# Ten of twelve pairs of token tiles: xn transposed on VectorE in 32x32 squares instead of on TensorE

## The chip, the cores and the metric

One core of one Trainium2 chip. The metric is the device time of one execution in microseconds (us).

## The reference, cut to what matters

An encoder block on 2048 + 1024 tokens of 1024 channels, all in float32. What matters here lies between the mixing and the FFN:

```
x = x + concat(ya, yb) @ w_out
h = rmsnorm(x, norm2_g)                      # x * rstd(x) * norm2_g
x = x + (silu(h @ w_gate) * (h @ w_up)) @ w_down     # D_FF = 2816
```

`rmsnorm` takes the mean square over the 1024 channels of a token; `norm2_g` is one weight per channel.

## The kernel before, in words

Every float32 matmul is three matmuls of rounded parts (hi x hi, lo x hi, hi x lo; lines 351 to 353, `three_products`). The rounded part is made by ScalarE, the rest by VectorE (`round_...` and `rest_of_...`). Large products use a scheme of seven products instead of eight (sums of halves before, sums of products after), so that both the weights and the moving data are needed as seven combinations.

The output projection (`project_out`) works on 24 tiles of 128 tokens. The first four tiles are done plainly; from then on two tiles are a pair, n = 2 to 11, and one pair is seven products of twelve matmuls (`pair`, `seventh`) on TensorE, in the order A11, S1, S2, A12, S3, S4, A22. The loop over pairs is written out by hand for each engine (`in_turn`, with pair LAST = 11 apart). While the products of pair n run, VectorE and ScalarE

- add the products of pair n to x (`u_sums`, `c11`, `c22`, `c12`, `c21`) in `x1`, which SP stores to `x1_scr` and fills anew with x for the next pair but one,
- prepare the seven combinations of y for pair n + 1 (`sum_v`, `round_v`, `rest_of_v`),
- and make h of pair n - 1. This is the part that the change is about: ScalarE squares a tile of x1 with its row sum (`squares`), VectorE and ScalarE make rstd from it (`variance`, `root`, `inverse`; lines 1835, 1623, 359 to 365), ScalarE writes xn = x1 * rstd (`scaled`, line 1627), TensorE transposes xn in eight squares of 128 into two PSUM banks (`transposes`, line 2020), ScalarE copies them to `h_out` and multiplies by norm2_g, which is one number per partition there (`stage_h`, line 1637), VectorE makes four sums of h's halves (`combine`, lines 1849 to 1854), and SP stores seven half-rows of h to `ha_scr` (`store_h`, lines 1529 to 1531).

Each engine runs its own instructions in the order in which they are written, and waits on semaphores. SP issues all of these DMAs, in its own order: per pair a store of x1, the load of y, a load of x, the second store of x1, the second load of x, and the stores of h. A load of x waits for the store of the same slot of x1 to have landed (`next_x`).

The FFN (`ffn`) reads seven 128x2048 blocks `a_raw` from `ha_scr` for each of three blocks of 1024 tokens, splits them into a_hi and a_lo (lines 2401 and 2592), and uses them as moving operand of 21 rounds of products. Its first tile is interleaved with the last pair of the output projection (`feed`).

Of the kernel before, what the change touches and what calls it, by code (L numbers as in the profile page):

```python
# [151 lines left out]
class Ahead:  # L152
# [4 lines left out]
    def __init__(self, nc, ctx):  # L157
# [699 lines left out]
class Mixer:  # L857
# [136 lines left out]
    def load_small(self, sp):  # L994
# [80 lines left out]
def mix(nc, ctx, ahead, mixer, z_scr, y_scr, w_pool):  # L1075
# [107 lines left out]
    def scalar(act):  # L1183
# [57 lines left out]
        for n in range(N):  # L1241
# [169 lines left out]
def project_out(nc, ctx, ahead, mixer, y_scr, x, x1_scr, ha_scr):  # L1411
# [19 lines left out]
    eye, gain2 = ahead.eye1, ahead.gain2  # L1431
# [35 lines left out]
    x1_stored, h_stored = ahead.x1_stored, ahead.h_stored  # L1467
# [35 lines left out]
    def sync(sp, feed):  # L1503
# [80 lines left out]
        store_h(LAST - 1, 0)  # L1584
# [3 lines left out]
        store_h(LAST, 1)  # L1588

    def scalar(act, feed):  # L1590
# [30 lines left out]
        def root(m, slot):  # L1621
            act.wait_ge(var_ready, m + 1)
            act.activation(std[:, slot:slot + 1], var[:, slot:slot + 1], ACT.Sqrt).then_inc(std_ready, 1)

        def scaled(m, slot):
            act.wait_ge(rstd_chain, m * 4 + 4)
            act.activation(xn[:, slot % 2, :], x1[:, slot, :], ACT.Copy, scale=rstd[:, slot:slot + 1]).then_inc(xn_ready, 1)  # L1627

        def stage_h(m, slot, stored=None):

            for half in range(2):
                act.wait_ge(transposed, m * 2 + (half + 1))
                if half == 0 and stored is not None:
                    act.wait_ge(*stored)
                for i in range(4):
                    d = 4 * half + i
                    out = act.activation(h_out[:, slot % 2, d, :], t_ps[(slot % 2) * 2 + half][:, i, :], ACT.Identity,  # L1637
                                         scale=gain2[:, d:d + 1])
                out.then_inc(h_staged, 1)
# [11 lines left out]
        act.wait_ge(ahead.gains_loaded, 2 * DMA)  # L1651
# [3 lines left out]
        root(0, 0)  # L1655
# [5 lines left out]
        root(1, 1)  # L1661
# [3 lines left out]
        stage_h(1, 1)  # L1665
# [1445 lines left out]
```

## Time and profile before

| | us |
|---|---|
| median of 3 runs | 2491.96 (2491.36 to 2492.42) |
| profiled execution, its own time | 2491.23 |
| its span | 2489.4 |
| TensorE busy (PE) | 2474.7 (99%) |
| VectorE busy (DVE) | 1676.6 (67%) |
| ScalarE busy (ACT) | 965.2 (39%) |

The page's 40 slices are 62.2 us each; the pairs of the output projection lie in slices 6 to 9 (375 to 557 us). TensorE's granted clock is 1.00 of full speed in every stretch shown. PE is TensorE, PEld its weight loads, SPq the queue of DMAs that SP issues. "Busy" of a matmul counts its whole duration, and matmuls overlap: one lasts 389 ns, and the next starts 227 ns after it.

### The profile page before, as it was taken

The page shows a single profiled execution, that of the slowest core. Times are in us where ns is not written, and L with a number is a line of the kernel's source. Part 1 is how long each engine was busy: PE and PEld are TensorE (multiplying, and loading weights), DVE is VectorE, ACT ScalarE, POOL GpSimd, SP SyncE. Part 2 cuts the span into 40 slices and gives each one's busy share as a digit, 9 for nine tenths or more (in the row PEclk, how much of TensorE's full clock was granted, in tenths as well). Part 3 has the DMA queues.
Part 4 walks back from the last instruction along what each step waited for, and adds up shares of the span by engine and source line. Part 5 has one row for each costly group of instructions (what it writes and reads, how often), then busy time and mean ns, then how long its engine had stood idle before and what let it go on. Part 6 is the DMA issues. An engine that isn't in the chain of part 4 may idle for free.

```text
span 2489.4 us, 32156 instructions
## 1 busy us (share of the span) xinstructions
PE 2474.7 (99%) x11141; PEld 2049.1 (82%) x11141; DVE 1676.6 (67%) x2600; ACT 965.2 (39%) x1830; POOL 166.9 (7%) x222
## 2 busy tenths in 40 slices
PE   9999999999999999999999999999999999999998
PEld 7888878887888888888888888888888888888887
DVE  5555788779767767877677687666774564455565
ACT  5534566667333333433333343333332232233333
POOL 2555400000000000000000000000000000000000
PEclk9999999999999999999999999999999999999999
DMA  6433767666423222532232432232346654354554
GB/s 184 115 85 99 223 221 254 238 238 260 157 80 116 97 103 110 195 113 110 80 126 101 155 146 96 110 110 89 118 186 217 242 200 168 119 196 149 195 189 148
DMA packets 154373, 381.99 MB, mean 153 GB/s; under 512 B 11992, under 2 KB 48184, under 8 KB 145076
## 3 DMA queue, kind: packets, MB, share of 16 engines
q1 hardware_dynamic: 145616, 350.81, 40.8%
q0 software_dynamic: 8240, 29.94, 3.2%
q8 instruction: 51, 0.84, 0.1%
q14 instruction: 34, 0.28, 0.0%
q10 hardware_dynamic: 432, 0.14, 0.0%
HBM read 254.22 MB, written 126.62 MB: 153 GB/s over the span
## 4 chain that ended last, share of the span: by engine, by line
PE 85%; DVE 2%; ACT 1%; issue 0%; DMA 0%; DVEq 0%
PE bank L351 28%; PE bank L353 28%; PE bank L352 28%; PE bank L2020 1%; ACT a_hi L2401 0%; DVE a_lo L2592 0%; DMA a_raw<-ha_scr 0%; PE bank L1373 0%; PE bank L1059 0%; DVE x L1818 0%; ACT h_out L1637 0%; DVE scratch L1033 0%; DVE zy_late L1044 0%; DVE uv_lo L1071 0%; ACT xn L1627 0%
## 5 line engine op out<-in xcount | busy, mean ns | idle before, releaser
L351 PE MATMUL bank<-a_hi,w_hi 128*128 128x512 f32 x1848 | 719.4, 389 | 2.0 <-DVE w_lo L2603 1.6
L352 PE MATMUL bank<-a_lo,w_hi 128*128 128x512 f32 x1848 | 718.9, 389 | 0.0
L353 PE MATMUL bank<-a_hi,w_lo 128*128 128x512 f32 x1848 | 718.9, 389 | 0.0
L351 PEld LDWEIGHTS bank<-a_hi,w_hi 128*128 128x128 f32 x1848 | 346.9, 188 | 75.6 <-DVE w_lo L2603 2.8
L353 PEld LDWEIGHTS bank<-a_hi,w_lo 128*128 128x128 f32 x1848 | 347.0, 188 | 72.0
L352 PEld LDWEIGHTS bank<-a_lo,w_hi 128*128 128x128 f32 x1848 | 347.0, 188 | 71.7
L351 PE MATMUL bank<-t_hi,s_hi 128*128 128x512 f32 x924 | 359.4, 389 | 0.0
L352 PE MATMUL bank<-t_lo,s_hi 128*128 128x512 f32 x924 | 359.4, 389 | 0.0
L353 PE MATMUL bank<-t_hi,s_lo 128*128 128x512 f32 x924 | 359.4, 389 | 0.0
L2414 ACT ACTIVATE w_hi<-t_raw 128x512 fp32r<-128x512 f32 x256 | 162.3, 634 | 462.4 <-PE bank L353 378.8
L2753 DVE TENSOR_TENSOR s_lo<-s_raw,s_hi 128x512 fp32r<-128x512 f32 x231 | 156.2, 687 | 230.7 <-ACT s_hi L2489 230.7
L2489 ACT ACTIVATE s_hi<-s_raw 128x512 fp32r<-128x512 f32 x231 | 133.8, 621 | 317.1 <-DMA s_raw<-s_scr 312.9
L351 PEld LDWEIGHTS bank<-t_hi,s_hi 128*128 128x128 f32 x924 | 173.4, 188 | 36.0
L353 PEld LDWEIGHTS bank<-t_hi,s_lo 128*128 128x128 f32 x924 | 173.4, 188 | 36.0
L352 PEld LDWEIGHTS bank<-t_lo,s_hi 128*128 128x128 f32 x924 | 173.4, 188 | 36.0
L2603 DVE TENSOR_TENSOR w_lo<-t_raw,w_hi 128x512 fp32r<-128x512 f32 x256 | 176.0, 688 | 29.9 <-ACT w_hi L2414 26.2
L2603 DVE TENSOR_TENSOR w_lo<-w_raw,w_hi 128x512 fp32r<-128x512 f32 x192 | 132.2, 688 | 87.7 <-ACT w_hi L2414 87.6
L2414 ACT ACTIVATE w_hi<-w_raw 128x512 fp32r<-128x512 f32 x192 | 120.6, 628 | 121.3 <-PE bank L353 121.0
L351 PE MATMUL bank<-h_hi,win_hi 128*128 128x512 f32 x380 | 149.6, 394 | 0.0
L353 PE MATMUL bank<-h_hi,win_lo 128*128 128x512 f32 x380 | 148.0, 389 | 0.0
L352 PE MATMUL bank<-h_lo,win_hi 128*128 128x512 f32 x380 | 148.0, 389 | 0.0
L2374 POOL DMA_DIRECT2D acc<-x_scr x6 | 4.5, 752 | 1641.1 <-PE bank L353 1641.1
(277 smaller groups left out, 3163.1 us busy)
## 6 DMA issues: line engine op xcount, KB each, us to landing
s_scr<-sums_out SPq DMA_DIRECT2D x33, 1792.0 KB, 5.9
s_raw<-s_scr SPq DMA_DIRECT2D x42, 1024.0 KB, 5.0
w_raw<-in_w_gate SPq DMA_DIRECT2D x64, 512.0 KB, 3.5
w_raw<-in_w_up SPq DMA_DIRECT2D x64, 512.0 KB, 4.3
wd_staged<-in_w_down SPq DMA_DIRECT2D x121, 256.0 KB
a_raw<-ha_scr SPq DMA_DIRECT2D x21, 1024.0 KB, 5.0
s_raw<-s_scr SPq DMA_DIRECT2D x21, 768.0 KB, 4.4
x<-in_x SPq DMA_DIRECT2D x24, 512.0 KB, 4.9
```

Source lines behind the costliest of these rows:

```text
L351: pe.matmul(out, w_hi, m_hi, start=first, stop=False, **checks)
L352: pe.matmul(out, w_hi, m_lo, start=False, stop=False, **checks)
L353: return pe.matmul(out, w_lo, m_hi, start=False, stop=last, **checks)
L2020: mm = pe.transpose(t_ps[(slot % 2) * 2 + k][:, i, :], xn[:, slot % 2, d * P:(d + 1) * P], eye[:, :])
L2374: pool.dma_start(acc[b][half][:, :, :], src).then_inc(acc_loaded[b][half], DMA)
L2414: act.activation(w_hi[j][:, :], src, ACT.Copy).then_inc(w_hi_done, 1)
L2489: act.activation(s_hi[c][:, k - 4 * c, :], s_raw[c][:, k - 4 * c, :], ACT.Copy).then_inc(s_hi_done, 1)
L2603: dve.tensor_tensor(w_lo[j][:, :], src, w_hi[j][:, :].bitcast(F32), ALU.subtract).then_inc(w_ready, 1)
L2753: dve.tensor_tensor(s_lo[c][:, k - 4 * c, :], s_raw[c][:, k - 4 * c, :], s_hi[c][:, k - 4 * c, :].bitcast(F32), ALU.subtract).then_inc(s_r ...
```

## The change

For pairs 1 to 10 (all but the first and the last) TensorE no longer transposes xn. After both tiles of a pair are scaled, VectorE transposes xn into `h_out`, one operation of 128x512 for each tile and half of the channels (`turn_squares`). It transposes each 32x32 square in its place, so partition 32 i + f of `h_out` holds channels of f, and tokens of the i-th group of 32. The columns are taken so that within `h_out` a partition's row holds, for each group m of 32 channels, four runs of 32 tokens. norm2_g is then one number per partition and square: ScalarE multiplies `h_out` in place by `gain_squares`, in 32 operations of 2 x 32 columns (`gains`). The stores of h bring the squares to their rows: one DMA for each group of 32 partitions and part, in pieces of 128 floats, twelve DMAs per pair instead of three (`store_squares`). `ha_scr` has its first two dimensions swapped. Inside a row of 512 the tokens now stand in another order, and the FFN reads its moving operand with a stride that undoes it (`tokens_of`). rstd is made for both tiles of a pair at once (`variance`, `root`, `inverse` on two columns), which goes with both `scaled` moving next to each other. `combine` moves to the end of a pair's work on VectorE. The first pair's h and the last pair's are still transposed by TensorE, and staged in the new token order. `gain_squares` is loaded early by four small DMAs.

```diff
@@ ScalarE @@
-        def stage_h(m, slot, stored=None):
+        def gains(n, a, first, last):
+            act.wait_ge(transposed, turned(n, a))
+            for b in range(first, last):
+                m, k = divmod(b, 4)
+                d = 4 * a + k
+                both = h_out[:, :, 4 * a + m, k * SQUARE:(k + 1) * SQUARE]
+                out = act.activation(both, both, ACT.Identity, scale=gain_squares[:, m, d:d + 1])
@@ ScalarE, pair @@
             round_v(after, k_after, 1 - par, A11)
-            scaled(n * 2 - 1, slot + 1)
-            stage_h(n * 2 - 2, slot, (h_stored[par], k * (3 * DMA)))
+            scaled(n, slot)
+            scaled(n, slot + 1)
             round_v(after, k_after, 1 - par, S1)
-            stage_h(n * 2 - 1, slot + 1)
-            for v in (S2, A12, S3):
-                round_v(after, k_after, 1 - par, v)
+            gains(n - 1, 0, 0, 16)
+            round_v(after, k_after, 1 - par, S2)
+            gains(n - 1, 1, 0, 8)
+            round_v(after, k_after, 1 - par, A12)
+            gains(n - 1, 1, 8, 16)
+            round_v(after, k_after, 1 - par, S3)
             squares(n * 2, 2 * par, n * 4 + 3)
             round_v(after, k_after, 1 - par, S4)
-            root(n * 2, 2 * par)
@@ ScalarE, last pair @@
-        round_v(LAST, NT // 4 - 1, 1, A22)
-        scaled(NT - 4, 0)
+        norms(LAST, NT // 4 - 1, 1)
+        scaled(LAST, 0)
+        scaled(LAST, 1)
         act.wait_ge(y_ready, split(LAST, A22))
         feed.round_a(0, 0)
-        squares(NT - 3, 1, LAST * 4)
-        root(NT - 3, 1)
-        copy_product(LAST)
-        scaled(NT - 3, 1)
-        stage_h(NT - 4, 0, (h_stored[1], (NT // 4 - 1) * (3 * DMA)))
+        gains(LAST - 1, 0, 0, 16)
         act.wait_ge(pair_ready, product_of(LAST, 2))
         feed.round_a(0, 1)
         feed.round_w(0, 0, 0, 0)
-        stage_h(NT - 3, 1)
+        gains(LAST - 1, 1, 0, 16)
@@ VectorE @@
+        def turn_squares(n, a, tile):
+            if (a, tile) == (0, 0):
+                dve.wait_ge(halves_out, halves_stored(n - 1))
+            if a == 0:
+                dve.wait_ge(xn_ready, n * 2 + (tile + 1))
+            half = xn[:, tile, a * HALF:(a + 1) * HALF].rearrange("p (k m f) -> p m k f", m=ROWS, f=SQUARE)
+            done = dve.transpose(h_out[:, tile, 4 * a:4 * a + 4, :].rearrange("p m (k t) -> p m k t", t=SQUARE), half)
+            if tile:
+                done.then_inc(transposed, 1)
@@ VectorE, last pair @@
-        c21(LAST - 1, 0)
-        for v in (A22, S3, S4):
-            rest_of_v(LAST, 1, v)
+        norms(LAST, 1)
         feed.rest_of_a(0, 0)
-        variance(NT - 3, 1)
-        inverse(NT - 3, 1)
+        for a in range(2):
+            for tile in range(2):
+                turn_squares(LAST - 1, a, tile)
         u_sums(LAST, rounds, 1)
@@ SP @@
-            sp.dma_start(ha_scr[0:2, b, :, q, :].rearrange("i p c -> p i c"), even).then_inc(h_stored[par], DMA)
-            sp.dma_start(ha_scr[2, b, :, q, :], odd).then_inc(h_stored[par], DMA)
-            sp.dma_start(ha_scr[3:7, b, :, q, :].rearrange("i p c -> p i c"), sums[:, :, :]).then_inc(h_stored[par], DMA)
+            for i in range(ROWS):
+                rows, cols = slice(i * SQUARE, (i + 1) * SQUARE), slice(i * P, (i + 1) * P)
+                sp.dma_start(ha_scr[b, 0:2, :, q, cols].rearrange("a (m f) c -> f (a m) c", f=SQUARE),
+                             h_out[rows, 0, :, :]).then_inc(halves_out, DMA)
+                sp.dma_start(ha_scr[b, 2, :, q, cols].rearrange("(m f) c -> f m c", f=SQUARE),
+                             h_out[rows, 1, 4:, :]).then_inc(halves_out, DMA)
+            sp.wait_ge(h_combined, n * 4 + 4)
+            for i in range(ROWS):
+                rows, cols = slice(i * SQUARE, (i + 1) * SQUARE), slice(i * P, (i + 1) * P)
+                sp.dma_start(ha_scr[b, 3:7, :, q, cols].rearrange("v (m f) c -> f (v m) c", f=SQUARE),
+                             h_sums[0][rows, :, :].rearrange("f v (m c) -> f (v m) c", m=ROWS)).then_inc(sums_out, DMA)
@@ TensorE @@
-            transposes(n * 2 - 2, slot)
             ready(S2, T2)
             seventh(S2)
-            transposes(n * 2 - 1, slot + 1)
@@ FFN, TensorE @@
+        def tokens_of(a, k):
+            return a[:, :, :].rearrange("p q (i k t) -> p (q i) k t", i=ROWS, t=SQUARE)[:, :, k, :]
-                mm = three_products(pe, ps[:, :], w_hi[j][:, cols], w_lo[j][:, cols], a_hi[slot][:, :, cols],
-                                    a_lo[slot][:, :, cols], k == 0 and not more, k == 3, skip_group_check=more)
+                mm = three_products(pe, ps[:, :], w_hi[j][:, cols], w_lo[j][:, cols], tokens_of(a_hi[slot], k),
+                                    tokens_of(a_lo[slot], k), k == 0 and not more, k == 3, skip_group_check=more)
```

The order of VectorE's instructions at the start of pair 3, before, from the last v_lo of pair 3's own combinations to `u_sum` (var, std, tmp and rstd are the steps of rstd, y_raw, v_raw and v_lo belong to the combinations of y for the next pair, bank1 and bank2 to the products of pair 3):

```order
L1780 TENSOR_TENSOR v_lo5_175<-v_raw5_182,v_hi5_168 128x512
L1835 TENSOR_SCALAR var3_151<-sumsq3_150 128x1
L359 RECIPROCAL tmp3_153<-std3_152 128x1
L361 SCALAR_TENSOR_TENSOR rstd3_154<-tmp3_153 128x1
L363 TENSOR_TENSOR rstd3_154<-rstd3_154,var3_151 128x1
L365 SCALAR_TENSOR_TENSOR rstd3_154<-rstd3_154,tmp3_153 128x1
L1780 TENSOR_TENSOR v_lo0_170<-y_raw0_51,v_hi0_163 128x512
L1775 TENSOR_TENSOR v_raw1_178<-y_raw0_51 128x512
L1775 TENSOR_TENSOR v_raw2_179<-v_raw1_178,y_raw0_51 128x512
L1780 TENSOR_TENSOR v_lo1_171<-v_raw1_178,v_hi1_164 128x512
L1800 TENSOR_TENSOR u_sum_184<-bank1,u_sum_184 128x512
```

and of the change, the same place:

```order
L1877 TENSOR_SCALAR var3_152<-sumsq3_151 128x2
L360 RECIPROCAL tmp3_154<-std3_153 128x2
L362 SCALAR_TENSOR_TENSOR rstd3_155<-tmp3_154 128x2
L364 TENSOR_TENSOR rstd3_155<-rstd3_155,var3_152 128x2
L366 SCALAR_TENSOR_TENSOR rstd3_155<-rstd3_155,tmp3_154 128x2
L1822 TENSOR_TENSOR v_lo0_171<-y_raw0_51,v_hi0_164 128x512
L1890 STREAM_TRANSPOSE h_out_98<-xn_148 128x512
L1817 TENSOR_TENSOR v_raw1_179<-y_raw0_51 128x512
L1890 STREAM_TRANSPOSE h_out_98<-xn_148 128x512 x3
L1817 TENSOR_TENSOR v_raw2_180<-v_raw1_179,y_raw0_51 128x512
L1822 TENSOR_TENSOR v_lo1_172<-v_raw1_179,v_hi1_165 128x512
L1842 TENSOR_TENSOR u_sum_185<-bank1,u_sum_185 128x512
```

Four transposes now stand ahead of `u_sum`, one before and three after v_raw1; the chain of rstd here works on two columns, and the other chain of a pair, which stood at its end, is gone (the four sums of h stand there now). SP, the stores of h of one pair and the DMA on either side, before:

```order
L1509 DMA x_96<-in_x 128x1024
L1529 DMA ha_scr<-h_out 128x2x512
L1530 DMA ha_scr<-h_out 128x512
L1531 DMA ha_scr<-h_sums_148 128x4x512
L1513 DMA x_scr<-x_96 128x1024
```

and of the change (the first two stores stand four times in turn):

```order
L1527 DMA x_97<-in_x 128x1024
L1557 DMA ha_scr<-h_out 32x8x128
L1559 DMA ha_scr<-h_out 32x4x128
L1564 DMA ha_scr<-h_sums_149 32x16x128 x4
L1531 DMA x_scr<-x_97 128x1024
```

Twelve stores stand where three stood, and the next store of x1 is behind them.

## Rows read from the trace of the kernel before

**Rows 1.** The page: busy us of each engine, share of the span, instructions

```profile
PE 2474.7 (99%) x11141; PEld 2049.1 (82%) x11141; DVE 1676.6 (67%) x2600; ACT 965.2 (39%) x1830; POOL 166.9 (7%) x222
```

**Rows 2.** By stretch: length, busy PE, PEld, DVE, ACT, POOL, clock, DMA share, GB/s

```profile
477.34:498.20 20.86, 20.86 (x103) 17.42 (x102) 16.43 (x35) 13.43 (x33) 0.00 (x0) 1.00 0.73 252
...
600.00:610.00 10.00, 8.69 (x46) 6.74 (x44) 9.93 (x10) 10.00 (x19) 0.00 (x0) 1.00 0.80 316
```

**Rows 3.** Timeline of TensorE: start us, us, engine, line, what

```profile
477.34 0.47 PE L351 MATMUL bank<-wout_hi,v_hi 128*128 128x512 f32 x1
...
485.63 0.39 PE L351 MATMUL bank<-wt_hi,v_hi 128*128 128x512 f32 x1
...
488.35 0.39 PE L351 MATMUL bank<-wout_hi,v_hi 128*128 128x512 f32 x1
...
498.20 0.47 PE L351 MATMUL bank<-wout_hi,v_hi 128*128 128x512 f32 x1
```

**Rows 4.** Timeline of VectorE in one pair

```profile
478.06 0.68 DVE L1800 TENSOR_TENSOR u_sum<-bank,u_sum 128x512 f32<-128x512 f32 x1
478.78 0.69 DVE L1802 TENSOR_TENSOR u_sum<-bank,u_sum 128x512 f32<-128x512 f32 x1
...
480.59 0.68 DVE L1810 TENSOR_TENSOR x<-x,u_sum 128x512 f32<-128x512 f32 x1
...
488.03 0.15 DVE L1835 TENSOR_SCALAR var<-sumsq 128x1 f32<-128x1 f32 x1
...
489.60 0.69 DVE L1818 TENSOR_TENSOR x<-bank,x 128x512 f32<-128x512 f32 x1 [0.21 <-DVE rstd L365]
```

**Rows 5.** VectorE's transposes of the first stage; weight loads (ns, min/median/max) of TensorE's

```profile
60.31 3.10 DVE L636 STREAM_TRANSPOSE x_turned<-xin 128x512 f32<-128x512 f32 x3
...
L718 PEld LDWEIGHTS bank<-eye,xin x16: 197/204/212, 18.9 to 29.1; 128*128 128x128 f32 x16
...
L2020 PEld LDWEIGHTS bank<-eye,xn x192: 138/140/143, 360.2 to 605.2; 128*128 128x128 f32 x192
```

**Rows 6.** Timeline of ScalarE in one pair; [idle before <- what ended it]

```profile
473.96 2.17 ACT L1637 ACTIVATE h_out<-bank,gain 128x128 f32<-128x128 f32 x8
...
486.24 0.63 ACT L1615 ACTIVATE v_hi<-v_raw 128x512 fp32r<-128x512 f32 x1 [5.22 <-DVE v_raw L1775]
...
492.19 0.20 ACT L1623 ACTIVATE std<-var 128x1 f32<-128x1 f32 x1 [0.57 <-DVE var L1835]
492.30 0.58 ACT L1643 ACTIVATE u_sum<-bank 128x512 f32<-128x512 f32 x1
493.30 1.14 ACT L1627 ACTIVATE xn<-x,rstd 128x1024 f32<-128x1024 f32 x1
```

**Rows 7.** Timeline of SP's DMA issues; two stretches, columns as rows 2

```profile
72.63 5.24 SPq L435 DMA_DIRECT2D xin<-in_x  x8
...
484.44 0.37 SPq L1529 DMA_DIRECT2D ha_scr<-h_out  x1
...
485.36 0.71 SPq L1531 DMA_DIRECT2D ha_scr<-h_sums  x1
...
491.88 0.33 SPq L1509 DMA_DIRECT2D x<-in_x  x1
...
75.00:79.50 4.50, 4.50 (x21) 3.72 (x20) 0.63 (x1) 4.50 (x23) 2.61 (x5) 1.00 1.22 226
583.00:589.00 6.00, 6.00 (x28) 4.94 (x27) 5.78 (x8) 4.47 (x11) 0.00 (x0) 1.00 1.02 408
```

**Rows 8.** Timeline of VectorE in the last pair

```profile
572.75 0.69 DVE L1818 TENSOR_TENSOR x<-bank,x 128x512 f32<-128x512 f32 x1
...
581.10 0.69 DVE L1800 TENSOR_TENSOR u_sum<-bank,u_sum 128x512 f32<-128x512 f32 x1 [1.70 <-PE bank L353]
...
584.51 2.29 DVE L2592 TENSOR_TENSOR a_lo<-a_raw,a_hi 128x2048 fp32r<-128x2048 f32 x1 [0.18 <-ACT a_hi L2401]
```

**Rows 9.** The page's costliest groups: matmuls of the FFN (busy us, mean ns)

```profile
L352 PE MATMUL bank<-a_lo,w_hi 128*128 128x512 f32 x1848 | 718.9, 389 | 0.0
```

More of the change, by code:

```diff
@@ L1247, in scalar @@
                 if SIDE[a] == "wp":
-                    act.wait_ge(ahead.gains_loaded, 2 * DMA)
+                    act.wait_ge(ahead.gains_loaded, (2 + ROWS) * DMA)
                 if SIDE[a][0] != "G":
@@ L1519, in next_x, with store_turned @@
             load_x(m + 4, slot)
-        def store_h(n, par):
-            last = isinstance(n, int) and n == LAST
+        def store_turned(n):
+            last = n == LAST
             b, q = n // 4, n % 4
@@ L1619, in squares, with root, scaled, stage_h @@
             act.activation(xn[:, slot % 2, :], x1[:, slot, :], ACT.Square, accum_out=sumsq[:, slot:slot + 1]).then_inc(squares_done, 1)
[L1621 to L1626, printed above, removed]
+        def root(number, tiles):
+            act.wait_ge(var_ready, number + 1)
+            act.activation(std[:, tiles], var[:, tiles], ACT.Sqrt).then_inc(std_ready, 1)
+        def scaled(number, slot):
+            act.wait_ge(rstd_chain, number * 4 + 4)
             act.activation(xn[:, slot % 2, :], x1[:, slot, :], ACT.Copy, scale=rstd[:, slot:slot + 1]).then_inc(xn_ready, 1)
-        def stage_h(m, slot, stored=None):
+        def stage_h(banks_done, tile):
             for half in range(2):
[L1632 to L1637, printed above, removed]
-                                         scale=gain2[:, d:d + 1])
+                act.wait_ge(transposed, banks_done + half + 1)
+                for k in range(4):
+                    d = 4 * half + k
+                    out = act.activation(h_out[:, tile, 4 * half:4 * half + 4, k * SQUARE:(k + 1) * SQUARE],
+                                         t_ps[2 * tile + half][:, k, :].rearrange("p (i t) -> p i t", t=SQUARE), ACT.Identity,
+                                         scale=gain2[:, d:d + 1])
+                out.then_inc(h_staged, 1)
+        def gains(n, a, first, last):
[5 more added lines that the diff above has]
+                out = act.activation(both, both, ACT.Identity, scale=gain_squares[:, m, d:d + 1])
+            if (a, last) == (1, 16):
                 out.then_inc(h_staged, 1)
@@ L1650, in scalar @@
         round_y(1)
-        act.wait_ge(ahead.gains_loaded, 2 * DMA)
+        act.wait_ge(ahead.gains_loaded, (2 + ROWS) * DMA)
         round_y(2)
@@ L1676, in norms @@
             round_v(n, k, par, A22)
-            scaled(n * 2 - 2, slot)
             squares(n * 2 - 1, slot + 1, n * 4)
-            root(n * 2 - 1, slot + 1)
+            root(n, slice(slot, slot + 2))
             copy_product(n)
@@ L1917, in pair @@
             c11(n, par)
-            if isinstance(n, int) and n == 2:
-                c22(n, par)
-                combine(n - 1, (h_stored[par], k * (3 * DMA)))
-            else:
-                combine(n - 1, (h_stored[par], k * (3 * DMA)))
-                c22(n, par)
+            c22(n, par)
             rest_of_v(after, 1 - par, A12)
@@ L1975, in combine_last @@
         def combine_last():
-            combine(LAST, None, last=True)
+            combine(LAST, staged(LAST - 1) + 4, last=True)
         feed.second_tile(combine_last)
@@ L2011, in products, with transposes @@
             mm.then_inc(tile_ready, 1)
-        def transposes(m, slot, first=False):
+        def transposes(m, tile):
             pe.wait_ge(xn_ready, m + 1)
             for k in range(2):
-                if not first:
-                    pe.wait_ge(h_staged, m * 2 + (k - 3))
                 for i in range(4):
                     d = 4 * k + i
-                    mm = pe.transpose(t_ps[(slot % 2) * 2 + k][:, i, :], xn[:, slot % 2, d * P:(d + 1) * P], eye[:, :])
+                    mm = pe.transpose(t_ps[2 * tile + k][:, i, :], xn[:, tile, d * P:(d + 1) * P], eye[:, :])
                 mm.then_inc(transposed, 1)
@@ L2069, in tensor @@
         products(1)
-        transposes(0, 0, first=True)
+        transposes(0, 0)
         products(2)
-        transposes(1, 1, first=True)
+        transposes(1, 1)
         products(3)
```

144 lines of the change are left out of this document (84 added, 60 removed).

## Prediction

> **What bounds the kernel now.** I read the page first: TensorE is busy 99% of the span [rows 1]. A change pays only if it takes work from TensorE, and only while nothing else then ends later. Next, the stretches of the output projection (about 340 to 557 us): in one pair of token tiles TensorE is busy for all of 20.86 us, VectorE for 16.43, ScalarE for 13.43, and the DMA engines have a share of 0.73 [rows 2]. The reader is to see there that three other resources have little room. The timeline of TensorE gives the parts of a pair: the same product starts at 477.34 and at 498.20, 20.86 us apart, and twelve matmuls (one of seven products) take 485.63 to 488.35, 2.72 us [rows 3]. Seven make 19.04 us; the remaining 1.82 us are the two sets of eight transposes of xn. Last, the stretch 600 to 610, where VectorE is busy 9.93 of 10 us, ScalarE 10.00, TensorE 8.69 [rows 2]: from the last pair into the first tile of the FFN the other two engines set the pace, so work given to them there is paid in full.
>
> **TensorE.** The transposes of ten pairs go, 160 of them: at most 10 x 1.82 = 18.2 us.
>
> **VectorE, per pair.** It now runs 24 operations of 512 columns. They start 0.60 us apart (three between 478.78 and 480.59), and 0.72 in the two places where one waits for its predecessor (478.06 to 478.78) [rows 4]: 22 x 0.60 + 2 x 0.72 = 14.6 us. It also runs two chains for rstd, the one shown from 488.03 to the next work at 489.60 [rows 4], 1.5 us each. The change keeps one chain (two columns at a time) and adds four transposes. Their price decides the case. Upper end: the transposes of the first stage have the same 128x512 shape, and three of them in a row take 3.10 us [rows 5], 1.03 each. But those read every fourth float of a row; the new ones read runs of 32 floats. Lower end: 0.60 apart, as any operation of 512 columns [rows 4]. That reading every fourth float costs an engine something is seen on TensorE: the weight loads of transposes take 204 ns from xin, read that way, and 140 ns from xn, read in one run [rows 5]. In reading, the new transposes are nearer to the contiguous operations, so I take 0.63 apart (0.71 long) and keep 1.03 for a rival. The Trainium skill says (Vector Engine (DVE) Microarchitecture Reference, 3.8) that the transpose array sustains one element per cycle per lane; by that the 1.03 would be due to the reading, and the sum would be mine. The trace of before has no transpose of contiguous data to show it.
>
> Sum: 14.6 + 1.5 + 4 x 0.63 = 18.6 us, and 0.45 of waiting, since both scaled tiles now come one after the other from ScalarE (1.14 each [rows 6], started 1.05 apart) and only one short operation lies between: 19.1 us, level with TensorE's 19.04. So a pair should take about 19.1 us.
>
> **ScalarE, per pair.** Sixteen copies of h out of PSUM go: eight of them take 2.17 us [rows 6], 0.27 each, 4.3 us. One root goes (0.1). In come 32 multiplications of 2 x 32 columns. Bounds: 0.11 (a root of one column, 492.19 to 492.30) and 0.27 (128 columns) [rows 6], so 3.5 to 8.7 us; about halfway, 0.2, gives 6.4. ScalarE comes to 13.4 + 2.0 = 15.4 of 19.1 us. They stand between the roundings that feed the next pair's products, in places where ScalarE idled 5.22 us before [rows 6]; that idle time covers the 2.0 us. At 0.27 it would no longer, and `combine`, behind them on VectorE, would hold up the next pair.
>
> **SP and the DMA queues, per pair.** h leaves in pieces of 512 B instead of 2 KB, and in twelve DMAs of 32 partitions instead of three of 128. Issuing: of the three, the first takes 0.37 and the largest 0.71 us; eight loads of xin, which have this form, take 5.24 us, 0.66 each [rows 7]. Eight smaller ones and four of that size are some 6 us of SP, 4.5 more; SP has room for it. Transfer: during the xin loads the engines move 226 GB/s at a share over 1, with another load of larger pieces among them; with large pieces alone 408 GB/s [rows 7]. I take 205 for the small ones. So the 1.83 MB of h (seven blocks of 128 x 512 floats) take 8.9 us instead of 4.5. The other 3.15 MB of a pair take 7.7. That is 16.6 of 19.1 us. But SP issues in order and waits twice per pair for a store of x1 before it reloads the slot. Before, stores of 2.36 MB issued from 484.44 on (5.8 us at 408 GB/s) let the waiting load go at 491.88 [rows 7], 7.44 us later: 1.6 us of landing. The loop now is: h 8.9, store of x1 1.3, landing 1.6, then 2.1 MB (y, x, second store) 5.1, landing 1.6, issue 0.4: 18.9 us. It is as long as the pair. I put 1 to 1.5 us in all on it. The other bound for unseen stores of this form: no dearer than the loads (gain kept), or a quarter slower (a rival). 
>
> **The tail.** There VectorE sets the pace. Before, c21 starts at 572.75, u_sum at 581.10 and the second a_lo at 584.51 [rows 8], 8.35 and 11.8 us later. Now the rounding of `a` stands behind both scaled tiles: c21 and three v_lo 2.4 us, rstd chain to 3.9, two xn to 6.0, a_hi (twice the columns of an xn, 1.9 as an estimate) to 7.9, a_lo (2.29 [rows 8], the next starts 0.1 before its end) to 10.2, four transposes to 12.7. So u_sum comes 12.7 us after c21 instead of 8.35. On ScalarE sixteen multiplications (3.2) and the next a_hi (1.9) follow the second transpose at 11.5, so the second a_lo starts at 16.6 instead of 11.8: 4.8 us lost. The last pair's removed transposes gain nothing here, as TensorE is ahead. So nine pairs count: 9 x 1.8 = 16.2 gained, 4.9 lost, 1 to 1.5 for the queue: **-10 us**. The new order of h's columns inside a row changes TensorE's moving operand of the FFN from runs of 128 floats to runs of 32; I cost it at nothing, since matmuls that read runs of 128 floats (a_lo [rows 9]) and of 512 (wt_hi, 485.63 [rows 3]) take 389 and 390 ns. A nanosecond on each of the 5,544 matmuls would be 5.5 us.
>
> The profiled execution is 2491.23 us (span 2489.4 and 1.8 around it), 0.7 under the median of 2491.96, against which I state everything: **2482 us**.
>
> **The rivals.**
> - A, the forecast: 2479 to 2486. Chance 0.40.
> - B, the store queue becomes the bound: h stores at 190 GB/s take 9.7 us, the loop 19.7, so 0.6 us a pair over nine pairs: 2487; at 170 GB/s the gain is gone, 2498. For it: the loop has no slack. Against it: 16.6 us of transfer in 19.1 is still not full. Chance 0.18.
> - C, on the other side: the new transposes cost what the old ones do, 1.03 each. VectorE then needs 14.6 + 1.5 + 4.1 + 0.45 = 20.65 us a pair and takes TensorE's place; a pair gains 0.2 us, nine pairs 2, and the tail loses 4.9 and 4 x 0.4 = 1.6 more: +4.5, 2496. It decides from about 0.9 us apart, where nine pairs of 20.86 - 16.55 - 4 x 0.9 no longer pay the tail. For it: the only measured transposes. Chance 0.33.
> - D, on the other side too, and by more: stores in 512 B pieces run slower than such loads. From 170 GB/s down they take back all; at 150 they need 12.2 us for h, loop 22.2, so 1.35 us a pair more than before over nine pairs, and the tail: +17, 2509. No row shows these stores. Chance 0.06.
> - E, the FFN's matmuls read slower, 3 ns each: 16.6 us lost against 10 gained, 2499. Chance 0.03.
> That the change does not do what it says is excluded by the order of instructions: the transposes stand on VectorE there.
>
> **How the numbers follow.** A measurement of this kernel tells about 0.2%, 5 us, from no change. Faster: nearly all of A (0.38) and half of B (0.10). Within 5 us: the rest of A and B (0.10), and most of C (0.24). Slower: the upper part of C (0.09), D and E. The range from 2478 to 2500 takes in A, B and C; A alone would be 2479 to 2486.
>
> **What would show it.** In the timeline of VectorE the new transposes start 0.63 apart (A, B) or 1.03 (C). A product of TensorE recurs every 19.1 us (A), with TensorE idle for 0.5 us or more before the products that wait for u_sum in C, and with VectorE's idle time ended by x or by the h stores in B. Multiplications of 64 columns last 0.15 to 0.25 us. The stretch of a pair shows a DMA share near 0.9. From the last pair's start to 620 the profile is some 5 us longer. The forecast is wrong if a pair lasts over 20 us, whatever the cause, or if FFN matmuls stand more than 227 ns apart.

## The result, and the profile after

| | us |
|---|---|
| median before | 2491.66 |
| median after | 2548.07 (2546.15 to 2552.46) |
| ratio | 1.0229, interval 1.0211 to 1.0246 |
| profiled execution after, its own time | 2552.46 |
| its span | 2550.7 |

The change makes the kernel 56 us slower. The forecast was 2482 us, 10 faster, and the range ended at 2500. The profiled execution is the slowest of the four, 4.4 us over the median, so the parts found in its trace add up to more than 56 us. The page's first part and the costliest matmul groups, which answer to [rows 1] and [rows 9]:

```profile
PE 2519.5 (99%) x10981; PEld 2036.2 (80%) x10981; DVE 1696.1 (66%) x2590; ACT 994.2 (39%) x1980; POOL 166.6 (7%) x222
...
L352 PE MATMUL bank<-a_hi,w_hi 128*128 128x512 f32 x1848 | 738.7, 400 | 0.9 <-DVE w_lo L2653 0.9
L354 PE MATMUL bank<-a_hi,w_lo 128*128 128x512 f32 x1848 | 738.6, 400 | 0.0
L353 PE MATMUL bank<-a_lo,w_hi 128*128 128x512 f32 x1848 | 735.9, 398 | 0.0
...
L353 PE MATMUL bank<-t_lo,s_hi 128*128 128x512 f32 x924 | 359.4, 389 | 0.0
```

TensorE is 99% busy in both kernels, and this is the trap of the page: its 160 removed instructions are gone from the count, and yet it is busy 45 us longer. The FFN's matmuls that read `a` went from 389 ns to 398 and 400; those of the last product, which do not read `a` (t_lo), kept 389. The stretch from 640 to 1000 us, all FFN, by windows (columns as in [rows 2]), after:

```profile
640.00:1000.00 360.00, 360.00 (x1523) 286.09 (x1522) 242.49 (x372) 109.18 (x181) 0.00 (x0) 1.00 0.27 98
```

and before:

```profile
640.00:1000.00 360.00, 360.00 (x1590) 298.19 (x1589) 252.72 (x389) 113.81 (x189) 0.00 (x0) 1.00 0.29 106
```

In the same 360 us at the same clock, 1,523 matmuls run instead of 1,590: one each 236.4 ns instead of 226.4. Over 5,544 matmuls, 10.0 ns are 55 us.

Splitting the 61.3 us between the two spans at the same instruction of both traces gives the account. The first u_sum of pair 2 starts at 397.00 (before 394.52), that of pair 10 at 560.23 (561.40), the FFN's first matmul at 600.3 (592.6), its last hi x hi matmul that reads `a` at 1914.9 (1853.7):

| stretch | forecast | measured |
|---|---|---|
| up to pair 2 | 0 | +2.5 |
| eight pairs, from pair 2 to pair 10 | 8 x -1.8 = -14.4 | -3.7 |
| pair 10 to the FFN's first matmul | +4.9 - 1.8 + 1 to 1.5 (queue) | +8.9 |
| FFN matmuls that read `a` | 0 | +53.5 |
| the rest | 0 | +0.1 |

The +2.5 us up to pair 2 are no more than executions differ by: the kernels of e4 and e12 below, which up to there are the kernel before, start pair 2 at 396.43 and 394.72. The second and third row vary too: e1 and e3 below, whose pairs are this kernel's, have -6.2 and -5.8 over the eight pairs and +7.7 and +7.4 behind them.

A pair recurs every 20.40 us (163.23 us over eight), not 19.1. The first two pairs last 19.36 and 19.29 us; from the third on it is 20.1 to 20.5, and 22.5 for the eighth. VectorE's timeline at the start of a pair:

```profile
490.62 0.69 DVE L1822 TENSOR_TENSOR v_lo<-y_raw,v_hi 128x512 fp32r<-128x512 f32 x1 [0.25 <-ACT v_hi L1649]
492.88 0.71 DVE L1890 STREAM_TRANSPOSE h_out<-xn 128x512 f32<-128x512 f32 x1 [1.57 <-DMA ha_scr<-h_out]
493.52 0.65 DVE L1817 TENSOR_TENSOR v_raw<-y_raw 128x512 f32<-128x512 f32 x1
494.09 1.89 DVE L1890 STREAM_TRANSPOSE h_out<-xn 128x512 f32<-128x512 f32 x3
```

Three transposes take 1.89 us: 0.60 apart and 0.7 long. They cost what I took them for. But the first waits 1.57 us until the previous pair's h has landed. SP's queue in the same pair:

```profile
479.55 0.43 SPq L1531 DMA_DIRECT2D x_scr<-x  x1
486.11 0.33 SPq L1527 DMA_DIRECT2D x<-in_x  x1
486.49 0.43 SPq L1557 DMA_DIRECT2D ha_scr<-h_out  x1
...
490.55 3.24 SPq L1564 DMA_DIRECT2D ha_scr<-h_sums  x4
493.83 0.70 SPq L1531 DMA_DIRECT2D x_scr<-x  x1
...
499.29 0.34 SPq L1527 DMA_DIRECT2D x<-in_x  x1
499.67 0.43 SPq L1531 DMA_DIRECT2D x_scr<-x  x1
```

and the chain that ended last, in the same stretch:

```profile
473.30 5.80 DMA x_scr<-x
...
479.55 6.50 DMA x_scr<-x
...
493.83 5.39 DMA x_scr<-x
...
499.67 6.64 DMA x_scr<-x
```

SP's loop in one pair (479.55 to 499.67, 20.1 us) is two landings of x1, 6.5 and 5.4 us, between them 7.3 us of issuing twelve stores, and 0.9 us of reloads and gaps. In it SP waits for nothing but landings. These landings are not longer than before the change: between 375 and 557 us the median from issue to landing of a store of x1 is 6.3 us, and was 6.9. New are the 7.3 us of issuing in line with them, where the three stores took 1.6 us (484.44 to 486.07). The first stores of h could have gone 3.4 us before 486.49, when ScalarE's last multiplication of h ended at 483.12, but they stand behind a reload that waits for a landing:

```profile
481.11 2.01 ACT L1681 ACTIVATE h_out<-h_out,gain_squares 128x64 f32<-128x64 f32 x8
```

In the last pair the waits between 560 and 600 us (total, times, longest), and one stretch of it by windows:

```profile
DVE a_lo L2642 <- ACT a_hi L2451: 9.4, 2, 5.3
PE bank L352 <- DVE x L1860: 7.6, 1, 7.6
PE bank L352 <- DVE u_sum L1844: 4.9, 2, 3.0
...
ACT a_hi L2451 <- DMA a_raw<-ha_scr: 3.6, 1, 3.6
```

```profile
590.00:595.00 5.00, 0.00 (x0) 0.00 (x0) 3.48 (x4) 4.43 (x13) 0.00 (x0) 0.50 1.02 428
```

The load of a_raw stands behind the twelve stores, ScalarE's a_hi waits for it, VectorE stands in `a_lo`'s wait for a_hi, and TensorE waits 7.6 us for the x that is queued behind. With TensorE idle, its granted clock is 0.50 there (1.2 GHz), and the timeline of TensorE goes on with matmuls of 0.63 us instead of 0.39, some 0.43 apart, so an idle stretch of TensorE is paid a second time:

```profile
595.15 0.77 PE L352 MATMUL bank<-wt_hi,v_hi 128*128 128x512 f32 x1 [7.56 <-DVE x L1860]
...
596.14 0.63 PE L354 MATMUL bank<-wt_hi,v_lo 128*128 128x512 f32 x1
596.57 0.63 PE L352 MATMUL bank<-wt_hi,v_hi 128*128 128x512 f32 x1
```

The twelve matmuls from 595.15 on take 5.2 us instead of 2.7. The same happens after the wait of 3.0 us for u_sum: the granted clock from 563 to 566 us is 0.50, with matmuls of 0.63 us. The kernel before has no such stretch here.

### The profile page after: what moved, and what is told of

The parts are those of the page before. It is cut to its first block, busy times and chain, and to the rows that moved or that the text cites. A ratio compares the mean times of both kernels' runs of the same rounds, so it can differ in the third digit from the quotient of the medians.

```text
span 2550.7 us, 31996 instructions
## 1 busy us (share of the span) xinstructions
PE 2519.5 (99%) x10981; PEld 2036.2 (80%) x10981; DVE 1696.1 (66%) x2590; ACT 994.2 (39%) x1980; POOL 166.6 (7%) x222
## 4 chain that ended last, share of the span: by engine, by line
PE 78%; DMA 4%; SPq 3%; DVE 2%; ACT 1%; issue 1%; DVEq 0%
PE bank L354 26%; PE bank L352 26%; PE bank L353 26%; DMA x_scr<-x 4%; SPq L1564 1%; SPq L1559 1%; SPq L1557 1%; ACT h_out L1681 0%; DMA w_raw<-in_w_up 0%; DVE a_lo L2642 0%; PE bank L1377 0%; SPq L1527 0%; PE bank L1063 0%; DVE v_lo L1822 0%; DVE zy_late L1048 0%
## 5 line engine op out<-in xcount | busy, mean ns | idle before, releaser
L352 PE MATMUL bank<-a_hi,w_hi 128*128 128x512 f32 x1848 | 738.7, 400 | 0.9 <-DVE w_lo L2653 0.9
L354 PE MATMUL bank<-a_hi,w_lo 128*128 128x512 f32 x1848 | 738.6, 400 | 0.0
L353 PE MATMUL bank<-a_lo,w_hi 128*128 128x512 f32 x1848 | 735.9, 398 | 0.0
L353 PEld LDWEIGHTS bank<-a_lo,w_hi 128*128 128x128 f32 x1848 | 348.4, 189 | 90.0
L354 PEld LDWEIGHTS bank<-a_hi,w_lo 128*128 128x128 f32 x1848 | 347.2, 188 | 90.6
L353 PE MATMUL bank<-t_lo,s_hi 128*128 128x512 f32 x924 | 359.4, 389 | 0.0
L354 PE MATMUL bank<-t_hi,s_lo 128*128 128x512 f32 x924 | 359.4, 389 | 0.0
L353 PEld LDWEIGHTS bank<-t_lo,s_hi 128*128 128x128 f32 x924 | 173.4, 188 | 36.0
L354 PEld LDWEIGHTS bank<-t_hi,s_lo 128*128 128x128 f32 x924 | 173.4, 188 | 36.0
L354 PE MATMUL bank<-h_hi,win_lo 128*128 128x512 f32 x380 | 148.0, 389 | 0.0
L353 PE MATMUL bank<-h_lo,win_hi 128*128 128x512 f32 x380 | 147.9, 389 | 0.0
```

Of the source, the lines that this page charges most:

```text
L352: pe.matmul(out, w_hi, m_hi, start=first, stop=False, **checks)
L353: pe.matmul(out, w_hi, m_lo, start=False, stop=False, **checks)
L354: return pe.matmul(out, w_lo, m_hi, start=False, stop=last, **checks)
```

## The experiments

Medians of "before" in these groups of runs are 2492.4 to 2492.5. All runs but e3, e10 and e11 give the FFN its tokens or channels in the wrong order (e8 leaves out weights too), so they compute another result and stand here for their time alone. The edits are shown in part: `...` marks what is left out, and semaphore increments are left out throughout.

**Which part costs the 56 us.** Two theories: R, reading the moving operand in runs of 32 floats; S, something else in the FFN. e1 undoes the reading alone, e2 does it alone.

```diff
@@ e1, in the change @@
-    tokens_of(a_hi[slot], k), tokens_of(a_lo[slot], k)
+    a_hi[slot][:, :, cols], a_lo[slot][:, :, cols]
@@ e2, in the kernel before @@
-    a_hi[slot][:, :, cols], a_lo[slot][:, :, cols]
+    tokens_of(a_hi[slot], k), tokens_of(a_lo[slot], k)
```

> The changed kernel, but the FFN's matmuls read 512 floats in four runs of 128, as before; the rows still hold the new token order, so the blocks of 128 channels are mixed and the FFN's result is another one. Everything ahead of the FFN and its DMAs is as in the change. Theory R (reading the moving operand in 16 runs of 32 floats costs 10 ns a matmul, x 5,544 = 55 us): about 2493 us, FFN matmuls 227 ns apart. Theory S (something else slows the FFN's matmuls, such as the other traffic, the clock, or later operands): 2546 us or little less, still 237 ns apart.

> The kernel before, in which only the FFN's matmuls read their 512 floats in 16 runs of 32 at a distance of 128 (each takes floats of four blocks of channels, so the FFN's result is another one). Theory R: 2492 + 55 = 2547 us, matmuls 237 ns apart, nothing else changed. Theory S: 2492.

Measured: e1 2494.68 us (ratio to before 1.001, 1.000 to 1.002), e2 2546.52 (1.0218, 1.0201 to 1.0235). That is 53.4 us less than the change and 54.1 more than before. The stretch from 640 to 1000 us of e1, then of e2:

```profile
640.00:1000.00 360.00, 360.00 (x1590) 298.38 (x1589) 253.47 (x391) 114.09 (x190) 0.00 (x0) 1.00 0.29 105
```

```profile
640.00:1000.00 360.00, 360.00 (x1522) 286.82 (x1522) 243.34 (x374) 109.27 (x182) 0.00 (x0) 1.00 0.27 99
```

The reading alone is the cause, in either kernel, and the whole rest of the change is worth +2 us (0 to 5 by the interval).

**How the price depends on the run.** The kernel before with runs of 64 (e4) and of 16 (e12); only `t` in `tokens_of` differs.

> The kernel before, in which the FFN's matmuls read 8 runs of 64 floats at a distance of 256 (the FFN's result is another one). If each run costs a fixed time beyond the first: four runs cost nothing visible against one (389 and 390 ns), 16 cost 10 ns, so 12 more runs cost 0.83 ns each and 8 runs 3.3 ns: 2492 + 18 = 2510 us. If there is a threshold between 32 and 128 floats: 2492 or 2547.

> The kernel before, in which the FFN's matmuls read 32 runs of 16 floats at a distance of 64 (the FFN's result is another one). Runs of 64 cost nothing, runs of 32 cost 9.8 ns a matmul. If a run costs a fixed time and part of it is hidden: 16 more runs cost more than the 9.8 ns, at 0.6 to 1.2 ns a run 20 to 30 ns in all, 2600 to 2655 us. If any run under 64 floats costs one fixed step per matmul: 2547 again.

Measured: e4 2492.51 us (0.9999, 0.999 to 1.0009), e12 2579.32 (1.035, 1.0333 to 1.0368). The window 640 to 1000 of e4, then of e12:

```profile
640.00:1000.00 360.00, 360.00 (x1590) 298.10 (x1589) 253.51 (x391) 114.20 (x190) 0.00 (x0) 1.00 0.29 105
```

```profile
640.00:1000.00 360.00, 360.00 (x1485) 281.12 (x1484) 236.45 (x362) 106.57 (x177) 0.00 (x0) 1.00 0.26 96
```

Eight runs of 64 floats: nothing. Sixteen of 32: 9.8 ns a matmul (54.1 us / 5,544). Thirty-two of 16: 15.7 ns (86.8 / 5,544). So it is neither a fixed time per run (e4 would be 2510, and e12 at least 2600) nor one step below 64 (e12 would be 2547). The straight line by the number of runs fell on both sides; a threshold between 32 and 128 floats is what e4 showed, and e12, which matched neither of its expectations, shows that the price below it still grows. The length of a run, the number of runs and the distance between them (256, 128 and 64 floats) changed together in these three runs, so which of them sets the price is not shown; "runs of 32" below stands for the whole pattern.

**Can the reading be mended cheaply.** e3: ScalarE reads a_raw in runs of 32 and writes a_hi in token order; a_lo is made in the place of a_raw and stays in the other order.

```diff
-    act.activation(a_hi[s][:, :, :], a_raw[s][:, :, :], ACT.Copy)
+    act.activation(in_order(a_hi[s]), by_block(a_raw[s]), ACT.Copy)
...
-    tokens_of(a_hi[slot], k), tokens_of(a_lo[slot], k)
+    in_order(a_hi[slot])[:, k, :, :], tokens_of(a_lo[slot], k)
```

> The changed kernel, with ScalarE writing a_hi in token order (it reads a_raw in runs of 32 and writes one run), so that two of three FFN matmuls read 512 floats in one run and only those of a_lo (1,848) read runs of 32. Theory R, cost by matmul and by reading: 2548 - 3,696 x 0.010 = 2511 us, a_hi matmuls 227 ns and a_lo matmuls 237 ns apart from the next; ScalarE's rounding of a block stays at 1.9 us if it reads runs of 32 for nothing. If the cost hung on the weights or on the sequence instead of on each matmul's own reading: 2548 or 2493.

Measured: 2524.10 us (1.0129, 1.0112 to 1.0146), 13 more than expected. The groups:

```profile
L353 PE MATMUL bank<-a_lo,w_hi 128*128 128x512 f32 x1848 | 737.3, 399 | 0.0
L354 PE MATMUL bank<-a_hi,w_lo 128*128 128x512 f32 x1848 | 729.4, 395 | 0.0
L352 PE MATMUL bank<-a_hi,w_hi 128*128 128x512 f32 x1848 | 723.1, 391 | 1.6 <-DVE w_lo L2665 1.5
...
L2463 ACT ACTIVATE a_hi<-a_raw 128x2048 fp32r<-128x2048 f32 x21 | 39.8, 1910 | 18.1 <-PE bank L354 13.2 <-DMA a_raw<-ha_scr 4.8
```

ScalarE reads runs of 32 for nothing (1,910 ns on average, and 1,910 without the edit). On TensorE, one third of the strided reads keeps 29.4 us of 53.4 (against e1), 15.9 ns each: the strided matmul (L353) lasts 399 ns instead of 389, and the one behind it (L354) 395, though it reads one run. Thinning out such reads pays less than in proportion.

**What holds a pair at 20.4 us.** Theory Q, the store queue (rival B of the prediction), against theory E, the hand-overs between VectorE and ScalarE (not the prediction's rival E). All on the kernel of e1. e5 stores h in three DMAs as before; e6 keeps twelve DMAs of 32 partitions, but in pieces of 2 KB; e8 leaves out 29 of the 32 multiplications.

```diff
@@ e5: store_squares @@
-    for i in range(ROWS): ...
+    sp.dma_start(ha_scr[b, 0:2, :, q, :].rearrange("i p c -> p i c"), even)
+    sp.dma_start(ha_scr[b, 2, :, q, :], odd)
...
+    sp.dma_start(ha_scr[b, 3:7, :, q, :].rearrange("i p c -> p i c"), h_sums[0][:, :, :])
@@ e6: store_squares, in the loop over i @@
+    even = h_out[rows, 0, :, :].rearrange("p (a k) c -> p a (k c)", a=2)
+    sp.dma_start(ha_scr[b, 0:2, rows, q, :].rearrange("i p c -> p i c"), even)
...
@@ e8: gains @@
-    for b in range(first, last):
+    for b in range(last - 1, last):
```

> The kernel of e1_read_runs_128 (2494.7 us, a pair 20.5 us), with h of the ten pairs stored as before the change: three DMAs of 128 partitions in pieces of 2 KB (the squares then lie in the wrong rows). Theory Q (a pair is bounded by the stores of h and what waits behind them: the halves' landing for the transposes, the landing of x1 for the reload): a pair 19.1 to 19.4 us, 9 x 1.2 = 11 us less, 2484; in the last pair the loads of a come earlier too, 2 to 4 us more, 2481. Theory E (VectorE and ScalarE set the pair through their hand-overs): 20.5 us a pair, 2494.

> The kernel of e1_read_runs_128, with the twelve DMAs of 32 partitions kept, but each in pieces of 2 KB instead of 512 B (the squares lie in the wrong rows). If the number of DMAs and their 32 partitions are what costs (issuing 7.3 us of SP): as e1, 2494. If it is the piece of 512 B: as e5, 2481 to 2484. Between them if both.

> The kernel of e1_read_runs_128, with three of the 32 multiplications by norm2_g per pair kept (the others are left out, so h lacks the weight in most squares). ScalarE then does 7 us less per pair. Theory Q or L: h is ready earlier, but SP issues its stores after the reload of x, so a pair stays at 20.3 to 20.5 us, 2492 to 2494. Theory E (ScalarE's 8 us of multiplications hold up the combinations of the next pair): 19.1 to 19.5 us, 2482 to 2486.

Measured (a pair of e1 is 20.09 us, the mean of eight between 19.3 and 21.1): e5 2485.68 us (0.9973, 0.9963 to 0.9983), a pair 19.32, each of the eight within 0.1; e6 2494.20 (1.0008, 0.9998 to 1.0018), a pair 20.13; e8 2495.23 (1.0013, 1.0003 to 1.0022), a pair 20.06. The queue holds the pair, ScalarE's new work does not, although it is 7 us of it. The piece of 512 B is not what costs: e6 moves pieces of 2 KB and is as slow as e1. From the second store of x1 to its reload, SP's rows of e5 and then of e6:

```profile
471.70 0.43 SPq L1531 DMA_DIRECT2D x_scr<-x  x1
477.03 0.33 SPq L1527 DMA_DIRECT2D x<-in_x  x1
```

```profile
476.86 0.43 SPq L1531 DMA_DIRECT2D x_scr<-x  x1
484.43 0.33 SPq L1527 DMA_DIRECT2D x<-in_x  x1
```

5.3 us and 7.6 (in the next pair 5.4 and 6.7). The twelve DMAs also issue for 7 us in line with the landings, where e5 needs 1.2, and that is the larger part. Which of the two, the number of DMAs or their 32 partitions, lengthens this landing was not parted. The Trainium skill (SBUF — State Buffer, Door 1: The DMA port swizzle) says that 32 partitions reach 8 of the 16 ports; no run here shows whether that plays a part.

**Latency or traffic.** e7 keeps every DMA of e1 and changes SP's order: both reloads of x first, then the next x1 even, h, x1 odd, each when its data is ready.

```diff
@@ SP, pair @@
-    store_x1(2 * n - 2, slot)
     sp.wait_ge(y_ready, split(n, A22))
...
     next_x(2 * n - 2, slot, before + 1)
-    store_x1(2 * n - 1, slot + 1)
     next_x(2 * n - 1, slot + 1, before + 1)
+    store_x1(2 * n, 2 * par)
     store_squares(n - 1)
+    store_x1(2 * n + 1, 2 * par + 1)
...
+store_x1(2, 2)
+store_x1(3, 3)
 for n in range(2, LAST):
...
-store_x1(NT - 4, 0)
-store_x1(NT - 3, 1)
```

> The kernel of e1_read_runs_128, with the same DMAs in another order on SP: both reloads of x ahead of the stores of h, and the two stores of x1 of the next pair around them, each where its data is ready (x1 even, h, x1 odd). Nothing on SP then waits for a landing behind h's stores. Theory L (latency: the loop of landings is too long, not the traffic): a pair 19.1 to 19.4 us, 2482 to 2484. Theory W (bandwidth: pieces of 512 B fill the queues): 20.3 us a pair, 2492 to 2494.

Measured: 2485.76 us (0.9974, 0.9964 to 0.9984), a pair 19.33. One pair of e7 by windows, SP's start of the stores, and VectorE at the transposes:

```profile
493.45:512.75 19.30, 19.30 (x85) 15.63 (x84) 17.97 (x35) 16.48 (x49) 0.00 (x0) 1.00 0.83 259
```

```profile
500.06 0.33 SPq L1531 DMA_DIRECT2D x_scr<-x  x1
500.44 0.42 SPq L1557 DMA_DIRECT2D ha_scr<-h_out  x1
...
504.76 2.98 SPq L1564 DMA_DIRECT2D ha_scr<-h_sums  x4
507.78 1.18 SPq L1531 DMA_DIRECT2D x_scr<-x  x1
```

```profile
488.22 0.69 DVE L1822 TENSOR_TENSOR v_lo<-y_raw,v_hi 128x512 fp32r<-128x512 f32 x1 [0.25 <-ACT v_hi L1649]
489.26 0.71 DVE L1890 STREAM_TRANSPOSE h_out<-xn 128x512 f32<-128x512 f32 x1 [0.35 <-ACT xn L1661]
```

The same bytes in the same pieces, still issued for 7.3 us, fit into 19.3 us: the pair was held by SP's order and the landings in it, and not by what the queues can carry. Now the transposes wait for xn, 0.35 us, and no longer for the stores.

The new order mends most of the last pair as well. From the first u_sum of pair 10 to the FFN's first matmul:

| kernel | us | against before |
|---|---|---|
| before | 31.2 | |
| the change | 40.1 | +8.9 |
| e1 | 38.9 | +7.7 |
| e5 | 36.2 | +4.9 |
| e7 | 34.9 | +3.7 |
| e9 (below) | 31.0 | -0.3 |

Without the queue's part the forecast for this stretch is 4.9 - 1.8 = +3.1. The second a_lo of e7 starts 17.0 us after c21 (561.68), where the forecast has 16.6 and the change 20.8 (570.73 to 591.51):

```profile
578.70 2.29 DVE L2642 TENSOR_TENSOR a_lo<-a_raw,a_hi 128x2048 fp32r<-128x2048 f32 x1 [1.51 <-ACT a_hi L2451]
```

**The last pair.** e9 is e7 with another order on VectorE:

```diff
-    feed.rest_of_a(0, 0)
     for a in range(2):
         for tile in range(2):
             turn_squares(LAST - 1, a, tile)
     u_sums(LAST, rounds, 1)
-    feed.rest_of_a(0, 1)
+    feed.rest_of_a(0, 0)
     c11(LAST, 1)
     c22(LAST, 1)
+    feed.rest_of_a(0, 1)
```

e10 is the change with the orders of e7 and e9 and a_hi as in e3. e11 is the change with the orders of e7 and e9 and a pass that sorts first:

```diff
@@ e11, ScalarE @@
-    act.activation(a_hi[s][:, :, :], a_raw[s][:, :, :], ACT.Copy)
+    act.activation(a_sorted[s][:, :, :].rearrange("p k (j t) -> p k j t", t=SQUARE),
+                   a_raw[s][:, :, :].rearrange("p q (i k t) -> p k (q i) t", i=ROWS, t=SQUARE), ACT.Copy)
+    act.activation(a_hi[s][:, :, :], a_sorted[s][:, :, :], ACT.Copy)
@@ e11, VectorE @@
-    dve.tensor_tensor(a_lo[s][:, :, :], a_raw[s][:, :, :], a_hi[s][:, :, :].bitcast(F32), ALU.subtract)
+    dve.tensor_tensor(a_lo[s][:, :, :], a_sorted[s][:, :, :], a_hi[s][:, :, :].bitcast(F32), ALU.subtract)
```

> The kernel of e7_store_order (2485.8 us; the FFN reads blocks of channels mixed), with another order on VectorE in the last pair: the four transposes and u_sums stand ahead of the first a_lo, and the second a_lo behind c11 and c22. Theory T (in the last pair PE waits because VectorE stands in a_lo's waits for ScalarE's a_hi, 4.1 us and 4.5 us, while x and u_sum are wanted): PE's waits of 2.9 us before the product that needs u_sum and 2.6 us before the one that needs x go, and 3 to 5 us are gained: 2481 to 2483. If instead the FFN's first tile is bound by VectorE's own work from there on, the time only moves: 2485 to 2486.

> The changed kernel's own result, with the stores' order of e7_store_order, the last pair's order of e9_order_and_tail, and a_hi written in token order as in e3_hi_in_order (only the a_lo matmuls read runs of 32). The parts measured so far add: 2524.1 - 8.9 (e7 against e1) - 0 to 5 (tail) = 2510 to 2515.

> The changed kernel's own result, with the stores' order of e7_store_order and the last pair's order of e9_order_and_tail, and a new pass on ScalarE: it first copies each block of a into token order (128x2048, about 1.9 us), then rounds a_hi from the copy, and VectorE makes a_lo from it, so that all FFN matmuls read 512 floats in one run. Theory R with free ScalarE time: no matmul reads runs of 32, -53 us; the pass costs nothing in the second and third block (ScalarE idle over 60%), and up to 7 x 1.9 = 13 us, as an estimate 5, in the first tile, where ScalarE was nearly full: 2484 to 2494.

Measured: e9 2484.39 us (0.9965, 0.9952 to 0.9977), e10 2513.82 (1.0084, 1.0068 to 1.0101), e11 2517.08 (1.0099, 1.0082 to 1.0116). TensorE's waits from 555 to 620 us in e7:

```profile
PE bank L352 <- DVE u_sum L1844: 2.9, 1, 2.9
PE bank L352 <- DVE x L1860: 2.6, 1, 2.6
PE bank L352 <- DVE w_lo L2653: 1.6, 2, 1.2
```

and in e9:

```profile
PE bank L352 <- DVE w_lo L2653: 4.9, 3, 3.4
PE bank L352 <- DVE a_lo L2642: 1.2, 1, 1.2
PE bank L352 <- DVE x L1860: 0.8, 1, 0.8
```

The wait for u_sum goes and that for x falls to 0.8, and the FFN's first matmul comes earlier, but most of the time moves to w_lo, which VectorE makes later: 1.4 us gained of the 3 to 5 expected, hardly clear of the scatter (2482.9 to 2485.1 against 2483.8 to 2488.7). e10 added up as forecast. e11 was a miss by 23 us: its matmuls are back at one each 226.4 ns (1,590 in the stretch from 640 to 1000 us), but where a block of `a` is exchanged ScalarE has 14 operations of 1.9 us to do in one tile, and TensorE waits. The group of e11:

```profile
L352 PE MATMUL bank<-a_hi,w_hi 128*128 128x512 f32 x1848 | 724.2, 392 | 31.6 <-ACT p L2479 12.3 <-DVE w_lo L2658 12.3 <-DVE c L2690 5.2
```

Of the 31.6 us, 12.3 are waits for w_lo in the first tile (4.9 in e9), and 17.5 come at the two later changes of block, where I had expected nothing. Behind such a wait the granted clock falls (0.52 from 1036 to 1042 us, for one, with matmuls of 0.63 us), so the mean here is 392 ns. I had counted ScalarE's idle share of a block (over 60%), not that of the one tile in which the seven blocks of `a` have to be exchanged. None of the versions that compute the block's result is faster than the kernel before: the best, e10, is 34 us below the change and 21 above before. Apart from the reading, what the change can bring is e9's 8 us.

## Why the prediction was wrong, point by point

- **The FFN's reading, "I cost it at nothing"**: this is the step that failed, and it holds 53 to 54 of the 66 us between forecast and result. The evidence was two widths, runs of 128 and of 512 floats at 389 and 390 ns, and I carried them on to 32, a width that no row showed. e4 shows that the line does go on to 64, e2 that it ends before 32. The text had worked out that a nanosecond was 5.5 us, more than half of the whole gain, and yet the rival (E, 3 ns each, chance 0.03) got neither the size nor the weight that such a lever asks for. It was the only part of the change that acts on 5,544 instructions of the engine that is always busy. Both of the signs by which the prediction said that it would be wrong came: FFN matmuls more than 227 ns apart (236.4), and a pair over 20 us (20.4). The Trainium skill (SBUF — State Buffer, Door 1: The DMA port swizzle) prices an engine's read by 16-byte lines, and a run of 32 floats has eight whole ones; by that rule such a read would cost no more than one in a single run, and the traces of e2 and e12 do not follow it.
- **TensorE, 1.82 us a pair**: right as an upper bound. Without the queue a pair went from 20.86 to 19.3 us, which gives 1.5.
- **VectorE, 19.1 us a pair**: right. Transposes 0.60 apart against 0.63, so rival C (1.03, chance 0.33) fell; the pair of e7 is 19.3, where TensorE's 84 matmuls alone would take 19.04 and VectorE's transposes wait only for xn. Which of the two engines sets the last 0.3 us was not parted. The Trainium skill (Vector Engine (DVE) Microarchitecture Reference, 3.8) gives one element per cycle and lane; the trace's 672 ns (median) for 512 columns is that of the other operations of this width, and agrees. That reading with a stride of four floats made the old ones slow remains a reading of two cases.
- **ScalarE, 0.2 us a multiplication**: mis-sized. Sixteen take 3.9 us, 0.24 each, 7.9 us a pair, near my upper bound of 0.27. I said that at 0.27 it would hold up the next pair; at 0.24 it does not: e8 gains nothing without them, and e7, with all 32 and the queue out of the way, has pairs of 19.3 us.
- **SP and the DMA queue, 18.9 us, "1 to 1.5 us in all"**: mis-sized, and for another reason than the one I priced. From the first store of h to the first reload the sum has 8.9 + 1.3 + 1.6 = 11.8 us, measured 12.8 (486.49 to 499.29); from there to the next store of h 7.1, measured 7.5 (to 506.75). The loop is 20.3 us and longer than the pair, not level with it. The 8.9 us were a price of the piece (205 GB/s for 512 B); e6 shows that pieces of 2 KB in twelve DMAs are no faster. So rival B happened in its effect, beside E: the queue bounds the pair, and VectorE's idle time is ended by the h stores, as B had it; its cause, the rate of small pieces, did not. Of 14.4 us expected over eight pairs it left 3.7 (6.2 in e1).
- **The tail, +4.9**: the chain was right. u_sum comes 12.3 us after c21 (forecast 12.7), and the second a_lo 20.8 us after it instead of 16.6. Of these 4.2 us, 3.6 are ScalarE's wait for a_raw, whose load stands behind the twelve stores, and 0.7 the sixteen multiplications (3.9 us instead of 3.2). With SP's order of e7 it is 17.0. What the sum left out is the queue's part in this stretch, and TensorE's clock of 0.50 after it had stood idle.

## What to carry to other kernels

A change of layout can be paid where the data is read more than where it is written: count how often each new access pattern is read on the bound engine, and measure that width before the rest is planned. TensorE's count of reads (5,544) times any price that can't be excluded belongs into the range. When an engine issues DMAs in order, put a reload that waits for a landing ahead of a batch of stores, and each store where its data becomes ready; here that alone took 20.1 us a pair (e1) to 19.3 (e7). The idle share of an engine over a long stage says little about the one tile in which work has to be exchanged.

## What the runs showed of the hardware that was not expected

- A matmul of 128x512 floats (read as fp32r) starts every 226.4 ns when its moving operand is read in runs of 64 or 128 floats, every 236.4 ns with 16 runs of 32 at a distance of 128, every 242.4 ns with 32 runs of 16 at a distance of 64 (360 us over 1,590, 1,523 and 1,485 matmuls; e4 and before, the change, e12).
- Mixed with contiguous ones, a strided read costs more than its share: 15.9 ns each with one in three (e3), 9.8 with all (e2). The matmul behind it is longer, 395 ns instead of 389.
- ScalarE's pass over 128x2048 floats costs nothing more when it reads in runs of 32: 1,910 ns on average in e3 and in the change alike.
- In stores of 32 partitions, pieces of 2 KB were no faster for the pair than pieces of 512 B (20.13 us in e6 and 20.09 in e1).
